# Decoder layer, one core: value columns and half of the output projection moved into the attention heads, values stacked high/low, keys in pairs, tiles on 64-byte starts

## The reference, cut to what matters

```python
u = rms_norm(h, attn_pre_g)
proj = u @ w_in                      # 1024 x 1952: c_q 256 | c_kv 128 | k_r 32 | moba q 512 | k 512 | v 512
mla_o = mla_attention(c_q, c_kv, k_r, ...)      # 8 heads: q up 256->96, k 64 + shared rotary 32, v 64, causal softmax
moba_o = moba_attention(rope(q), rope(k), v)    # 8 heads of 64; with 512 tokens and top 3 of 2 blocks of 256: plain causal attention
h = h + rms_norm(concat(mla_o, moba_o) @ w_out, attn_post_g)
a = square(relu(rms_norm(h, mlp_pre_g) @ w_up)) # 1024 -> 4096
h = h + rms_norm(a @ w_down, mlp_post_g)
```

## Time and profile before

| | |
|---|---|
| median of 3 runs | 616.59 us (616.37 to 616.63) |
| the profiled execution's own time | 616.86 us |
| its span in the profile | 614.9 us |
| granted clock of TensorE, mean | 0.997 |
| busy: PE / PE weight loads / DVE / ACT / POOL | 98% / 81% / 48% / 44% / 16% |
| from HBM | 52.8 MB, 89 GB/s over the span |

### The profile page before, as it was taken

One profiled execution on the slowest core, in us unless ns is written; L12 is line 12 of the kernel. 1 busy time (PEld: TensorE's weight loads), 2 busy tenths in 40 slices (PEclk: granted clock), 3 DMA queues, 4 the chain that ended last, 5 costly groups with the idle time before them and its releaser, 6 DMA issues.

```text
span 614.9 us, 8201 instructions
## 1 busy us (share of the span) xinstructions
PE 601.3 (98%) x2992; PEld 501.1 (81%) x2992; DVE 296.7 (48%) x587; ACT 268.1 (44%) x564; POOL 100.7 (16%) x167
## 2 busy tenths in 40 slices
PE   7999999999999999999999999999999999999996
PEld 7988888877787788998888888888888888888874
DVE  3458582788788308534534335352422423323244
ACT  5563252789898324355344253442313213123132
POOL 1153200445797101120000000000000000000011
PEclk9999999999999999999999999999999999999998
DMA  8442412000220174004242322414241232321203
GB/s 300 126 131 60 164 69 68 1 1 1 70 70 1 42 266 138 0 1 137 68 136 68 114 91 77 128 68 136 70 136 68 74 130 68 102 103 68 103 22 115
DMA packets 32826, 55.24 MB, mean 90 GB/s; under 512 B 3232, under 2 KB 21408, under 8 KB 32800
## 3 DMA queue, kind: packets, MB, share of 16 engines
q1 hardware_dynamic: 31760, 54.90, 26.6%
q10 hardware_dynamic: 1040, 0.00, 0.1%
HBM read 52.80 MB, written 2.10 MB: 89 GB/s over the span
## 4 chain that ended last, share of the span: by engine, by line
PE 93%; DVE 2%; ACT 2%; DMA 1%; issue 1%; SPq 0%; DVEq 0%; POOLq 0%; POOL 0%; ACTq 0%
PE bank L913 30%; PE bank L915 29%; PE bank L914 29%; PE bank L1083 2%; DMA x_sb<-in_x 1%; ACT probs L501 1%; DVE pT_lo L635 1%; DVE bank L767 1%; PE bank L1020 1%; PE bank L919 1%; PE bank L952 1%; PE bank L1036 0%; ACT pT_hi L389 0%; PE bank L978 0%; ACT uT_hi L389 0%
## 5 line engine op out<-in xcount | busy, mean ns | idle before, releaser
L913 PE MATMUL bank<-uT_hi,w_hi 128*128 128x512 f32 (+1 forms) x280 | 104.0, 371 | 0.0
L914 PE MATMUL bank<-uT_lo,w_hi 128*128 128x512 f32 (+1 forms) x280 | 103.8, 371 | 0.0
L915 PE MATMUL bank<-uT_hi,w_lo 128*128 128x512 f32 (+1 forms) x280 | 103.8, 371 | 0.0
L913 PE MATMUL bank<-w_hi,a_hi 128*128 128x512 f32 x256 | 101.2, 395 | 0.0
L914 PE MATMUL bank<-w_lo,a_hi 128*128 128x512 f32 x256 | 101.1, 395 | 0.0
L915 PE MATMUL bank<-w_hi,a_lo 128*128 128x512 f32 x256 | 101.1, 395 | 0.0
L635 DVE TENSOR_TENSOR w_lo<-w_raw,w_hi 128x2048 fp32r<-128x2048 f32 (+1 forms) x17 | 38.4, 2260 | 116.3 <-ACT w_hi L389 116.3
L389 ACT ACTIVATE w_hi<-w_raw 128x2048 fp32r<-128x2048 f32 (+2 forms) x25 | 37.0, 1490 | 123.2 <-PE bank L915 122.4
L638 DVE SCALAR_TENSOR_TENSOR w_lo<-w_raw,g_up,w_hi 128x256 fp32r<-128x256 f32 x128 | 52.0, 479 | 49.3 <-ACT w_hi L389 49.3
L322 POOL TENSOR_SCALAR stat<-stat 128x1 f32<-128x1 f32 x8 | 1.8, 229 | 369.4 <-ACT junk_post L414 369.4
L599 ACT ACTIVATE relu<-bank 128x512 f32<-128x512 f32 x32 | 19.1, 598 | 98.2 <-PE bank L915 98.2
(11 more groups left out here) (127 smaller groups left out, 925.0 us busy)
## 6 DMA issues: line engine op xcount, KB each, us to landing
w_raw<-in_w_up SPq DMA_DIRECT2D x16, 1024.0 KB, 5.5
w_raw<-in_w_down SPq DMA_DIRECT2D x16, 1024.0 KB, 4.8
w_raw<-in_w_in SPq DMA_DIRECT2D x6, 1024.0 KB, 5.9
w_raw<-in_w_out SPq DMA_DIRECT2D x4, 1024.0 KB, 4.9
x_sb<-in_x SPq DMA_DIRECT2D x8, 256.0 KB, 6.2
h_sb<-in_x SPq DMA_DIRECT2D x4, 512.0 KB, 5.9
out<-h_sb SPq DMA_DIRECT2D x8, 256.0 KB, 2.0
w_raw<-in_w_in SPq DMA_DIRECT2D x2, 416.0 KB, 5.3
```

The costliest lines, as they stand in the source:

```text
L913: nc.tensor.matmul(out, lh, rh, start=start, stop=False)
L914: nc.tensor.matmul(out, lh, rl, start=False, stop=False)
L915: return nc.tensor.matmul(out, ll, rh, start=False, stop=stop)
```

## The change

The value columns of the input (`group(3)`) leave the start and half of the output projection leaves the end; both run as "filler" in the head steps. The four row blocks of `w_out` for the MLA heads (k = 0 to 3) are used early, with their sums copied to `y_part` and added back (`added`); k = 4 to 7 come last. Values are stacked as 64 high and 64 low columns of one stationary operand, so that `weighted` is two matmuls per key block and the two halves of the result are added by ACT and DVE (`o_part`); POOL splits the sum of two heads (`split_pair`). Keys of two MLA heads come from one `mm3`. The weights for q and kv are loaded before MoBA k's; the MoBA q and k rotation reads SBUF copies (`natural`) instead of PSUM. `half` lies inside `stat`, a filler tile brings the next start to 5120 bytes, and every tile starts on a multiple of 64. `pT` has one buffer instead of two. The core of the diff:

```diff
-    IN_CH = [0, 1, 2, 3, 4, 5, 8, 9]
-    Q_CH, KV_CH = 6, 7
+    IN_CH = [0, 1, 2, 3, 6, 7, 8, 9]
+    Q_CH, KV_CH = 4, 5
+    OUT_K = [4, 6, 0, 2]
...
+        half = stat[:, 4, 0, 1:2]
+        fill_to_1k = sb("fill_to_2k", [P, (5120 - 4480) // 4])
...
+        Q_LATE = {i: i + 2 for i in range(HEADS - 2)}
+        K_EARLY = {1: 2, 3: 4, 5: 6}
+        MOBA_PREP = {6: 8, 8: 10, 10: 12, 12: 14}
+        V_HALVES = range(0, 2 * NT)
+        OUT_UNITS = range(NH + 2 - 2 * NT, NH + 2)
-        OUT_PIECES = {i: [i - 4] if i < HEADS else [2 * i - 12, 2 * i - 11] for i in range(4, 14)}
+        OUT_PIECES = {6 + c: [PIECES * c + n for n in range(PIECES)] for c in range(4)}
+        DVE_PIECES = {8: (8, 9), 9: (12, 13)}
```

ACT's head loop after the change (DVE's is the same with `maxes` and `inverse_sums` for `exps`, without `natural`, and with `DVE_PIECES`):

```diff
+            for i in range(NH + 2):
+                if i >= 2:
+                    p_part(i - 2, 2)
+                if i - 1 in V_HALVES and i % 2 == 0:
+                    v_part(i // 2 - 1)
+                if i - 1 in OUT_UNITS:
+                    out_part(i - 1 - OUT_UNITS[0])
...
+                if i < NH:
+                    exps(i, S_ORDER)
...
+                if i in K_EARLY:
+                    k_part(K_EARLY[i], PREP)
+                if i in MOBA_PREP:
+                    q_part(MOBA_PREP[i], PREP)
                 for n in OUT_PIECES.get(i, []):
                     out_piece(n)
                 if i >= 2:
                     o_part(i - 2)
+                if 1 <= i <= NH:
+                    p_part(i - 1, 0)
+                    p_part(i - 1, 1)
+                if i in Q_LATE:
+                    q_part(Q_LATE[i], PREP)
+                if i in MOBA_PREP:
+                    k_part(MOBA_PREP[i], PREP)
```

DVE behind the two `mlp_lo` of the first up chunks, which stay where they were, as do SP's wait for `o_full` and its order:

```diff
+            for t in range(NT):
+                added(t)
+                if t == 0:
+                    dve.wait_ge(g_post_in, 16)
+                if t >= 2:
+                    transposed_lo(2 * NT, t - 2)
                 dve.wait_ge(h_in[t], 16)
+                scaled(t)
+            for t in range(2, NT):
+                transposed_lo(2 * NT, t)
```

PE:

```diff
+            def last_T(i):
+                pe.wait_ge(pl, 3 * i + 1)
+                probs_T(i, 2).then_inc(pT_full, 1)
...
                 for k in range(NT):
                     w = slice(PT_OFF[k], PT_OFF[k] + P * (NT - k))
+                    v = (v_mla, v_moba)[i // HEADS][:, k, i % HEADS, :, :]
+                    nc.tensor.matmul(ps[O][:, P * k:TOP], v, pT_hi[:, w], start=k == 0, stop=False)
+                    last = nc.tensor.matmul(ps[O][:, P * k:TOP], v, pT_lo[:, w], start=False, stop=k == NT - 1)
...
+            for i in range(NH + 2):
+                if 1 <= i < NH:
+                    scores(i)
+                if i in K_EARLY:
+                    pe.wait_ge(ql, i + 2)
+                    k_prep(K_EARLY[i], PREP)
+                if i in MOBA_PREP:
+                    pe.wait_ge(*((ql, HEADS) if i == 6 else (kl, k_preps(MOBA_PREP[i]) - 1)))
+                    q_prep(MOBA_PREP[i], PREP)
+                filler(i, 0)
+                if i >= 2:
+                    weighted(i - 2)
+                if 1 <= i <= NH:
+                    first_T(i - 1)
+                filler(i, 1)
...
+                if i in MOBA_PREP:
+                    pe.wait_ge(ql, q_preps(MOBA_PREP[i]))
+                    k_prep(MOBA_PREP[i], PREP)
+                if 1 <= i <= NH:
+                    last_T(i - 1)
...
+            for t in range(1, NT):
...
                 for b in range(2):
+                    if t == NT - 1 and b == 1:
+                        pe.wait_ge(h_ready, 4)
+                        transposes(h_sb, 1)
+                    out_final(t, b, range(4, 8)).then_inc(y_full, 1)
+                if t == 2:
+                    pe.wait_ge(h_ready, 2)
+                    transposes(h_sb, 0)
```

More of the change, by code:

```diff
@@ L759, in maxes @@
+            in_lo(5)
             def maxes(i, tiles):
@@ L793, in p_part, with q_part @@
-            def p_part(i):
-                for n, (b, c, w) in enumerate(PT_COPY):
-                    dve.wait_ge(ph, 3 * i + n + 1)
-                    lo_part(pT_lo[i % 2][:, c:c + w], ps[b][:, 0:w], pT_hi[i % 2][:, c:c + w]).then_inc(pl, 1)
+                    nc.vector.reciprocal(rs[:, i % 2, w], rs[:, i % 2, w]).then_inc(s_ri, 1)
+            def q_part(i, bank):
+                dve.wait_ge(qh, q_preps(i))
+                rows, s = QH if i < HEADS else P, slot(i)
+                lo_part(qT_lo[s][0:rows, :], ps[bank][0:rows, :], qT_hi[s][0:rows, :]).then_inc(ql, 1)
@@ new lines, in _ @@
+            k_part(0, 0)
+            q_part(0, 1)
+            q_part(1, 2)
+            in_lo(6)
+            for i in range(NH + 2):
+                if i >= 2:
+                    p_part(i - 2, 2)
+                if i - 1 in V_HALVES and i % 2 == 0:
+                    v_part(i // 2 - 1)
+                if i == 0:
+                    turn_two(NT)
+                if i < NH:
+                    maxes(i, S_ORDER)
+                    inverse_sums(i)
+                if i == 0:
+                    turn_two(NT + 2)
+                    in_lo(7)
+                if i in K_EARLY:
+                    k_part(K_EARLY[i], PREP)
+                if i in MOBA_PREP:
+                    q_part(MOBA_PREP[i], PREP)
+                for n in DVE_PIECES.get(i, ()):
+                    out_piece(n)
@@ L922, in transposes, with in_rows @@
                         last.then_inc(uT_full, 1)
+            def in_rows(bank, g, part, t, ks):
+                n, r, tok = GROUP_COLS[g][1], IN_CH[2 * g + part], slice(P * t, P * t + P)
+                for k in ks:
+                    if r == 0 and t == 0 and k >= 1:
+                        pe.wait_ge(*((first_ready, k + 1) if k < 3 else (w_ready, 1)))
+                    w = slice(n * k, n * k + n)
+                    last = mm3(ps[bank][:, 0:n], uT_hi[:, 4 * part + k, tok], uT_lo[:, 4 * part + k, tok],
+                               w_hi[w_slot(r)][:, w], w_lo[w_slot(r)][:, w], part == 0 and k == 0, part == 1 and k == 3)
+                return last
             def group(g, before_tile):
-                n = GROUP_COLS[g][1]
                 for part in range(2):
@@ L1140, in _, with out_rows @@
[L1140 to L1155 removed]
+            def out_rows(bank, t, b, k, first, final):
+                c, tok = OUT_K.index(k - k % 2), slice(P * t, P * t + P)
+                hi, lo = out_tiles(c)
+                m_hi, m_lo = mix(k)
+                w = slice(D * (k % 2) + TOP * b, D * (k % 2) + TOP * b + TOP)
+                return mm3(ps[bank][:, :], m_hi[:, k, tok], m_lo[:, k, tok], hi[:, w], lo[:, w], first, final)
```

811 lines of the change are left out of this document (419 added, 392 removed).

## The result

The changed kernel takes **642.33 us** (median of 4 runs, 640.27 to 643.8) against 616.61 (4 runs beside it): ratio 1.0415, 95% interval 1.0385 to 1.0446. It is slower, as forecast, but by 25.7 us where 6.6 were forecast, and outside the range. The profiled execution, the longest of the four (643.8), has a span of 641.9, 20.3 over the 621.6 of the forecast's sum.

The account below looks back on a forecast made before the run. PE was taken to bound the kernel, standing still 10.7 us in the heads. Terms -2.8 - 7.7 - 6.2 - 10.7 + 12.8 + 19.8 + 1.5 = +6.7 on a 614.9 span gave a 623.2 us median; range 614.5 to 629.

Parts of the forecast that it names:

- the joint: Between last head and up projection: PE waits for DVE's first sum, queued behind mlp_lo, then for DVE's loop; +19.8 us.
- the clock: Granted clock falls to 1.2 GHz in PE's idle stretches between heads and up projection; +1.5 us, bounds 0 and +6.
- Rival D: Between heads and up projection, x and up chunks land earlier, PE's wait shrinks by 6 to 7: 616.5 us; chance 9%.
- alignment: In 512-column matmuls, mainly the down projection, an operand starting 32 bytes off costs 0.0067 us each; removing it gives -6.2 us.
- Rival C: The 0.0067 us per matmul has another cause than 32-byte starts and stays: 629 us; chance 6%.
- stacked values: In each head, two value matmuls per key block instead of three: 1.27 us instead of 1.75, together -7.7 us.
- Terms 1 and 2: Keys of MLA heads prepared in pairs, -2.8 us; values stacked in one stationary operand, -7.7 us.
- term 4: In the heads, fillers take off 10.7 us of PE standing still; moved work costs the same; new waits add 12.8.
- rival B: Waits in steps 8 and 9 also drop the clock, lengthening these steps, and the joint pays twice: +4, 627 us; 17%.
- Steps 6 to 9: PE's last_T waits behind ACT's weight pieces; steps last about 9.0, 7.9, 9.1, 8.0 us: +1.2, +1.0, +4.0, +3.8.
- Rival A: In steps 6 to 9 last_T isn't late, as ACT fits the pieces into its waits: 613 us, faster; chance 13%.
- Steps 1, 16 and 17: Step 1's key preparation waits for its bank behind q_part(2), +1.9 us; no wait was walked for the other two.

Follow-up runs that it names:

- e4: The changed kernel with the split of the first two up chunks moved into the residual loop and up block 0 started on the first chunk alone: 623.05 us.
- e1: The kernel before with two pads, so that operands start on a multiple of 64 bytes: 610.75 us, ratio 0.9905.
- e2: The changed kernel with every tile behind the filler tile, so every split operand, starting 32 bytes past a multiple of 64: 642.41 us, ratio 1.0424.
- e8: The changed kernel with the half output projection taken out of steps 10 to 17 and run right behind the heads: 649.25 us, ratio 1.0518.
- e6: The changed kernel with small matmuls keeping PE busy ahead of two waits between the heads and the up projection: 640.13 us, ratio 1.0392.
- e9: The changed kernel with small matmuls keeping PE busy in the waits of steps 1, 7, 8 and 9: 639.53 us, ratio 1.0363.
- e15: The changed kernel with weight pieces behind the copies, e4's order, filler copies first, and e9's small matmuls: 612.9 us, ratio 0.9948.
- e3: The changed kernel with the output weight pieces put behind the copies o_part and p_part on ACT and DVE: 635.57 us, ratio 1.0306.
- e11: The changed kernel with e3's and e4's orders, last_T behind the next scores, and step 1's first_T(0) and filler ahead of the key preparation: 636.55 us.

## Why the prediction was wrong

**Right: the sign, the joint, everything behind it.** The joint's waits were forecast as 12.0, 2.2 and 5.6, and came as 11.5, 0.5 and 5.1; the A blocks end at +57.2 behind the last values against +55.2. e4 confirms the cause and the size (19.3, with the joint's share of the clock in it, against 19.8 and 1.5 of clock). Rival D is out.

**Right: alignment, by size.** 6.2 forecast, 5.8 measured (e1). The Trainium skill (SBUF — State Buffer, Operand start alignment) treats starts as a matter of legality and says that its runs timed nothing; the runs here show a price, and one that depends on two operands together. My reason was half right, since e2 shows that an operand off 64 costs nothing by itself. Rival C is out.

**Right, a little better than forecast: stacked values.** A head's values take 1.22 us (109.50 to 110.72 in the kernel after), where 1.27 were forecast and 1.75 stood before; behind a score instead of a filler they take 1.34 (e8). Terms 1 and 2 have no run of their own. Timeline of PE:

```profile
109.50 0.40 PE L1223 MATMUL bank<-pT_hi,v_mla 128*128 128x512 f32 x1
...
110.61 0.28 PE L1224 MATMUL bank<-pT_lo,v_mla 128*128 128x128 f32 x1
110.72 0.40 PE L1190 MATMUL bank<-ident,probs 128*128 128x128 f32 x2
```

**Wrong: term 4, the heads, and in it two steps.** The forecast took 10.7 us of standing still off and put 12.8 of new waits on. The first step that failed is the count of work: what PE does in a step was priced too low, and "moved work costs the same". The second is the new waits, which were too small and carried next to no clock. Of the 19.5 us that were missing:

- *The work of a step was counted too small, and so the idle time to be filled too large.* "14 scores at 1.9 us" fits no MoBA head. In the kernel before the scores of MLA heads take 1.91 to 2.00, unhindered ones of MoBA heads 2.11 (at 154.06); after, 1.99 and 2.10 (0.80, 0.35, 0.28, 0.67). For the 14 scores of the sum that makes 2.1 us which were work. The earlier trace rows held the warning: in their 91.0 us PE is shown idle for 4.3, where my sum had 10.7 in 97.3; a shown length reaches some 0.16 over the next start, so the eleven waits of that stretch hide up to 2 more (an estimate from these rows), not 6. In the 15 scores of the new steps the difference is 2.2. Fillers pay for being cut in as well. Here the first of six, and the last score before it:

```profile
206.97 0.34 PE L1033 MATMUL bank<-kT_hi,qT_lo 64*128 64x384 f32 x1
207.24 0.50 PE L1031 MATMUL bank<-w_hi,cT_hi 128*128 128x512 f32 x1
207.57 0.39 PE L1032 MATMUL bank<-w_lo,cT_hi 128*128 128x512 f32 x1
207.81 0.39 PE L1033 MATMUL bank<-w_hi,cT_lo 128*128 128x512 f32 x1
```

  0.33 to the second start, 0.24 to the third. A filler behind transposes, a q or k preparation, a MoBA score or a wait takes 1.46 to 1.50, not 1.36; directly behind another product of the same shape it keeps 1.36 (116.26). 26 of the 32 pay, at 0.11: 2.9. "Moved work costs the same" was wrong by this much. Together 5.1 us, read from the traces; no run took it away, and what makes the first matmul slower isn't shown.
- *The clock.* The term was 1.5 in all, and rival B, falls in steps 8 and 9, was priced at 4. It happened, in steps 1, 8, 9 and 10, and the joint pays 3.4 by itself (e6, by profiled executions: its shortest against this kernel's longest). In the heads 3 to 6 us (e9, e15).
- *Steps 6 to 9.* With most of the half clock gone 37.2 (e9) against 34.0: the mechanism was walked correctly and is 3.2 dearer, of which 0.9 is the scores and fillers counted above. With the pieces moved it is 33.5 (e3). Rival A is out.
- *Steps 1, 16 and 17.* 3.2 of wait instead of 1.9, and twice 1.1 for `out_part` behind the copy of `last_T`, which I had not walked at all: 3.5.

These make 14 to 17 of 19.5; the rest I can't name.

**What the forecast did not ask** is what a two-bank head does without fillers (e8): a step takes 6.6 at least, where 5.5 to 5.9 stood before.

**What stays open.** e15 is at 612.9 with 4.9 us of waits and 9.3 of small matmuls still in its heads, where the kernel before with even starts, e1, is at 610.75. No version of the change that I ran beats it. Key pairs and stacked values without moved work, on the three-bank head and even starts, was not tried.

## What to carry to other kernels

Work moved into another stage's idle time costs something extra each time it is cut in (0.11 us for each filler of 1.36 here), and the resource it takes there, a bank or a place in another engine's program, may make part of the idle time that it then fills: measure the stage with the resource taken and the work left out. Before moving work out of a stretch, list what it was covering: here a stretch without cover was worth 19 us, and they came back from reordering the engines' programs (e4). When a wait is removed by moving an instruction, look at what is queued behind its consumer on the copying engine; the wait often only changes its place.

## What was not expected of the hardware

- Speed of a matmul depends on where moving and stationary operands start relative to each other: 0.2267 us with both on a multiple of 64 bytes or both 32 past one, 0.2333 with one of each (512 columns; e1, e2).
- The first filler matmul (512 columns) behind transposes, a preparation, a MoBA score or a wait starts its successor after 0.31 to 0.34 us instead of 0.23; directly behind a product of the same shape (116.26, 132.83) it doesn't, nor behind the MLA scores of step 7 (150.69).
- In the kernel after, with a wait of PE of 3.2 us (94.8 to 98.0) came 6.8 us at a granted 1.2 GHz, which began inside the wait; with waits of 1.2 and 2.9 close together (step 8) 10.3; behind one of 2.2 (step 9) 6.8; behind single waits of 1.6 and 1.3 (steps 6 and 7) none. In e8, waits of at most 1.7 us in every step came with a mean clock of 0.75 from 178 to 234.
- The runs of kernels with falls of the clock in their heads or joint spread over 2 to 6 us (e11, with its one long run, over 10); those of the kernel before over 0.7, of e1 over 0.4.
